# Two heads at a time: where in the gate units the second head's scores and both weightings stand, and output sums in two banks

## What is computed, cut to what matters

```python
h = rms_norm(x, norm)                         # 256 x 2048
q, k, v, g = h @ w_q, h @ w_k, h @ w_v, h @ w_g   # each 256 x 4096, 32 heads of 128
sc = q @ k.T * 128 ** -0.5 + bias_or_decay    # per head, masked
p = softmax(sc)
o = p @ v
x = x + (o * silu(g)) @ w_out
```

## Time and profile before

| what | value |
|---|---|
| device time, median of 3 runs | 2803.97 us (2802.63 to 2807.37) |
| the profiled execution, its own time | 2815.8 us |
| span of its records | 2814.1 us |
| PE busy | 2618.1 us, 93% |
| PE weight loads | 2283.6 us, 81% |
| DVE busy | 1823.2 us, 65% |
| ACT busy | 1303.0 us, 46% |
| POOL busy | 347.6 us, 12% |
| mean granted clock of PE | 0.966 |
| read from HBM | 437.35 MB |

### The profile page before, as it was taken

One profiled execution on the slowest core, in us unless ns is written; L12 is line 12 of the kernel. 1 busy time (PEld: TensorE's weight loads), 2 busy tenths in 40 slices (PEclk: granted clock), 3 DMA queues, 4 the chain that ended last, 5 costly groups with the idle time before them and its releaser, 6 DMA issues.

```text
span 2814.1 us, 43733 instructions
## 1 busy us (share of the span) xinstructions
PE 2618.1 (93%) x15162; PEld 2283.6 (81%) x15162; DVE 1823.2 (65%) x2629; ACT 1303.0 (46%) x2054; POOL 347.6 (12%) x375
## 2 busy tenths in 40 slices
PE   7999996888899999999999999999999999999997
PEld 6999993776788788888878888788888788888886
DVE  6888887347865656665565656666655666565565
ACT  5454446354444444444444445544444444444444
POOL 3111117231300000000000000110000101000012
PEclk9999998798999999999999999999999999999999
DMA  6666640007566565656656565557666666666672
GB/s 190 181 164 185 167 125 17 14 4 207 167 176 177 157 185 155 184 166 168 176 152 181 167 168 151 168 148 193 171 163 182 159 191 162 170 176 179 170 172 90
DMA packets 757372, 441.72 MB, mean 157 GB/s; under 512 B 28304, under 2 KB 720528, under 8 KB 757296
## 3 DMA queue, kind: packets, MB, share of 16 engines
q1 hardware_dynamic: 752016, 430.16, 54.7%
q0 software_dynamic: 5280, 10.56, 3.5%
HBM read 437.35 MB, written 3.31 MB: 157 GB/s over the span
## 4 chain that ended last, share of the span: by engine, by line
PE 61%; DVE 6%; ACT 6%; issue 3%; ACTq 0%; DVEq 0%; DMA 0%; POOL 0%; SPq 0%; POOLq 0%
PE bank L271 30%; PE bank L273 15%; PE bank L295 4%; PE bank L296 4%; PE bank L297 4%; ACT hib L231 4%; PE bank L1540 1%; ACT pr L1633 1%; DVE lob L238 1%; DVE gT L1783 1%; PE bank L1541 1%; DVE gT L1781 1%; DVE egT L1812 1%; DVE og L1814 0%; PE bank L1521 0%
## 5 line engine op out<-in xcount | busy, mean ns | idle before, releaser
L271 PE MATMUL bank<-xx,hib 128*128 128x512 f32 x3328 | 1221.2, 409 | 10.5 <-DVE lob L238 10.5
L238 DVE TENSOR_TENSOR lob<-rawb,hib 128x1024 fp32r<-128x1024 f32 x672 | 827.4, 1244 | 443.5 <-ACT hib L231 437.7
L273 PE MATMUL bank<-xx,lob 128*128 128x256 f32 x3328 | 941.3, 283 | 0.0
L231 ACT ACTIVATE hib<-rawb 128x1024 fp32r<-128x1024 f32 x672 | 699.1, 1054 | 516.6 <-PE bank L273 353.4
L271 PEld LDWEIGHTS bank<-xx,hib 128*128 128x128 f32 x3328 | 634.1, 191 | 159.7 <-DVE lob L238 11.2
L273 PEld LDWEIGHTS bank<-xx,lob 128*128 128x128 f32 x3328 | 637.3, 192 | 2.3
L271 PE MATMUL bank<-oo,hib 128*128 128x512 f32 x1024 | 367.9, 404 | 14.5 <-DVE gT L1783 12.8
L254 PE MATMUL bank<-xh,hia 128*128 128x258 f32 (+2 forms) x1040 | 299.5, 288 | 12.2 <-DVE xl L413 12.2
L255 PE MATMUL bank<-xl,hia 128*128 128x258 f32 (+2 forms) x1040 | 295.9, 284 | 0.0
L256 PE MATMUL bank<-xh,loa 128*128 128x258 f32 (+2 forms) x1040 | 294.9, 284 | 0.0
L273 PE MATMUL bank<-oo,lob 128*128 128x256 f32 x1024 | 289.4, 283 | 0.0
(11 more groups left out here) (303 smaller groups left out, 2648.2 us busy)
## 6 DMA issues: line engine op xcount, KB each, us to landing
rawb<-in_a_w_in_dram SPq DMA_DIRECT2D x256, 512.0 KB, 4.6
rawa<-in_w_in_dram SPq DMA_DIRECT2D x130, 512.0 KB, 5.0
rawb<-in_kv_w_dram SPq DMA_DIRECT2D x128, 512.0 KB, 4.6
rawb<-in_b_w_in_dram SPq DMA_DIRECT2D x128, 512.0 KB, 5.2
rawb<-in_a_w_out_dram SPq DMA_DIRECT2D x64, 512.0 KB, 5.1
rawb<-in_b_w_out_dram SPq DMA_DIRECT2D x64, 512.0 KB, 5.1
rawb<-in_w_out_dram SPq DMA_DIRECT2D x32, 512.0 KB, 5.4
table<-in_rel_dram POOLq DMA_DIRECT2D x32, 128.0 KB, 3.5
```

Of the source, the lines that this page charges most:

```text
L231: nc.scalar.activation(self.hi[(2 * at.u + h) % SPL][:], self.raw[at.u % RAW][:, h * HALF:(h + 1) * HALF], ACT.Copy).then_inc(hi_ready, 1)
L238: nc.vector.tensor_tensor(self.lo[b][:], self.raw[at.u % RAW][:, h * HALF:(h + 1) * HALF], self.hi[b][:].bitcast(F32), ALU.subtract).then_ ...
L271: nc.tensor.matmul(out, self.hi[b][:, w], both(k).rearrange("p a t -> p (a t)"), start=start and k == 0, stop=False)
L273: last = nc.tensor.matmul(out[:, 0:SEQ], self.lo[b][:, w], both(k)[:, 0], start=False, stop=stop and k == 7)
```

## The change

In each pair of heads, PE issues the second head's scores and then the first head's weighting together ahead of tile 6 of g_a's first half, the second head's transposes ahead of tile 6 of g_b's first half, and its weighting ahead of tile 6 of g_b's second half. The sums of even heads go to the bank OT and those of odd heads to FZ, which the norms' sums use between the layers, and the semaphore `og_ready` starts one higher, so that a weighting waits for the og of the head before the last. ACT copies the second head's turned probabilities after the first head's tanh and ahead of its copy of og, which is now a step of its own (`take_gated`); the splits of g_b follow both. DVE takes the second head's maxima between the two splits of g_a.

```diff
@@ buffers @@
     SC, PT, OT, FZ = psum[2:6]
+    OUTS = [OT, FZ]
@@ TensorE, weigh @@
-                            nc.tensor.matmul(OT[:, 0:SEQ], vtm[:, 0, w], pT[:, 0:SEQ], start=True, stop=False)
-                            nc.tensor.matmul(OT[:, P:SEQ], vtm[:, 1, w], pT[:, SEQ:W3], start=False,
+                            nc.tensor.matmul(OUTS[j % 2][:, 0:SEQ], vtm[:, 0, w], pT[:, 0:SEQ], start=True, stop=False)
+                            nc.tensor.matmul(OUTS[j % 2][:, P:SEQ], vtm[:, 1, w], pT[:, SEQ:W3], start=False,
                                              stop=True).then_inc(o_sum, 1)
+                        return emit
+                    def both(one, other):
+                        def emit():
+                            one()
+                            other()
                         return emit
@@ TensorE, the pair @@
-                        st.unit_wide(pe, g_a, xg, ({4: weigh(j_a)}, {0: scores(j_b, q_b, k_b)}))
-                        st.unit_wide(pe, g_b, xg, ({}, {0: turn_probs(j_b), 5: weigh(j_b)}))
+                        st.unit_wide(pe, g_a, xg, ({6: both(scores(j_b, q_b, k_b), weigh(j_a))}, {}))
+                        st.unit_wide(pe, g_b, xg, ({6: turn_probs(j_b)}, {6: weigh(j_b)}))
@@ ScalarE, gate @@
                         a(eg[:], gT[:], ACT.Tanh, scale=0.5).then_inc(gate_ready, 1)
-                        act.wait_ge(og_ready, head_no(layer, g, b, j) + 2)
+
+                    def take_gated(j):
+                        act.wait_ge(og_ready, head_no(layer, g, b, j) + 3)
                         dst = oo[:, bass.ds(b * VB + j, 1), 0, :].rearrange("p a t -> p (a t)")
                         a(dst, og[:], ACT.Copy).then_inc(oh_ready, 1)
...
-                    act.wait_ge(og_ready, head_no(layer, g, b, 0) + 1)
+                    act.wait_ge(og_ready, head_no(layer, g, b, 0) + 2)
@@ ScalarE, the pair @@
                         split(g_a)
                         exps(j_b)
                         gate(g_a, j_a)
+                        take_probs(j_b)
+                        take_gated(j_a)
                         split(g_b)
-                        take_probs(j_b)
                         gate(g_b, j_b)
+                        take_gated(j_b)
@@ VectorE, start @@
-            v_.memset(stat[:, 1:2], 0.0).then_inc(og_ready, 1)
+            for n in range(1, 3):
+                v_.memset(stat[:, n:n + 1], 0.0).then_inc(og_ready, 1)
@@ VectorE, gate @@
-                        stt(og[:], OT[:, 0:SEQ], 0.5, eg[:], ALU.mult, ALU.mult).then_inc(og_ready, 1)
+                        stt(og[:], OUTS[j % 2][:, 0:SEQ], 0.5, eg[:], ALU.mult, ALU.mult).then_inc(og_ready, 1)
@@ VectorE, the pair @@
                         evacuate(p, U_KB, k_b, kT)
-                        split(g_a)
+                        ahead(split_lo, g_a, 0)
                         maxima(j_b)
+                        ahead(split_lo, g_a, 1)
                         shares(j_b)
```

## The result

The changed kernel takes 2692.69 us (median of 4 runs, 2690.08 to 2697.28), the kernel before 2803.67 in the same comparison. The ratio is 0.9604, 95% interval 0.9587 to 0.9621: 111 us less. The forecast was 2707 with a range of 2692 to 2738, so the time lies 0.7 us above the range's lower end: the direction and the mechanism were right, and the gain was 14 us larger than the 97 of the sum.

A forecast was written before the change was run, and what follows sets the result against it. The prediction saw PE bound by waits for ACT's late pT copy and by clock falls beside them. Removing 71.9 us of wait and 25 us of clock, 97 us in all, took 2804 to 2707 us, range 2692 to 2738.

The forecast's parts named there:

- The wait of 71.9 us: PE's second-head weighting waits for ACT's pT copy, 2.25 us in each of 32 pairs; the change removes it.
- The schedule of the new order: Predicted start times of one pair's steps on PE, ACT and DVE, with pT 2.1 us before the second weighting.
- The thinnest margin: Second head's scores on PE need kT, forecast ready 0.6 us before them.
- A second bank worth nothing by itself: Weighting no longer waits for og of the head before; claimed worth nothing, as og came before PE was ready.
- Maxima between the splits: DVE's maxima between g_a's splits start exp 2.0 us earlier; probabilities ready 1.7 us before PE's transposes.
- The wait at the group ends: First projection matmul of each of 8 head groups waits for gT; claimed untouched at 12.8 us.
- The clock: Falls of PE's clock at the pair waits were expected to go: 33 us at most, 25 us taken.
- Two discounts: Clock gain cut from 33 to 29 us for the profiled run's 11.8 us excess, then by 4 for group-end falls.
- Rival 1: Clock falls stay, caused by the short fp32 matmuls or transposes around the wait; 2732 us, chance 0.14.
- Rival 2: New PE wait for kT at the second head's scores, 1 us late per pair; 2739 us, chance 0.09.
- Rival 3: ACT's pT copy still late behind gated copy or splits, wait returns in full; 2804 us, chance 0.04.
- Rival 4: Weight loads too slow for the shorter pair, PE waits at a unit's start; 2855 us, chance 0.03.

The follow-up runs named there:

- experiment 1: Kernel before with only ACT's order changed: pT copy after tanh, ahead of the gated copy and the splits of g_b; 2714.48 us, ratio 0.9669.
- experiment 2: Changed kernel with ACT's pT copy of the second head put back behind the splits of g_b; 2710.48 us, ratio 0.9644.
- experiment 5: Kernel of experiment 2 with the second weighting at tile 2 instead of 6 of g_b's second half; 2752.98 us, ratio 0.9816.
- experiment 6: Kernel of experiment 2 with the second weighting at tile 0 instead of 6 of g_b's second half; 2807.28 us, ratio 1.0014.
- experiment 3: Changed kernel with all heads' sums in one bank and the weighting waiting for og of the head before; 2695.23 us, ratio 0.9596.
- experiment 4: Changed kernel with DVE's second-head maxima put back behind both splits of g_a; 2730.3 us, ratio 0.9716.
- experiment 7: Changed kernel without PE's wait for gT of the last head at the start of a group's projection; 2684.38 us, ratio 0.9565.
- experiment 8: Kernel of experiment 1 without PE's wait for gT at the start of a group's projection; 2684.61 us, ratio 0.9571.

## Why the prediction was right, point by point

- **The wait of 71.9 us and its cause, ACT's queue.** Right. Experiment 1 removes it with ACT's order alone, experiments 2, 5 and 6 bring it back in three sizes.
- **The schedule of the new order.** Right to a few hundredths of a microsecond. On the clock of the prediction the rows after are: scores 1098.76 (forecast 1098.76), exp 1101.94 (1102.0), the probabilities 1103.96 (1104.0), transposes 1105.72 (1105.73), tanh 1105.13 (1105.1), og 1106.04 (1106.0), pT 1106.24 (1106.3), splits of g_b 1106.94 (1107.0), second weighting 1108.87 (1108.88). The thinnest margin, kT before the scores, is 1075.73 - 1075.10 = 0.63 us, forecast 0.6.
- **A second bank worth nothing by itself.** Right (experiment 3).
- **Maxima between the splits.** The margin of 1.7 us at the transposes was right. Moved back, the maxima cost a wait of 0.72 us per pair and, by way of the group ends, 37.6 us in all (experiment 4).
- **The wait at the group ends stays at 12.8 us.** Right, but the reason was incomplete. It stays because the splits of g_b became earlier along with g_b's end; had they not, it would have grown (experiment 1).
- **The clock.** The mechanism was right, and this is the term that was mis-sized. I took 25 us; the missing share fell by 34.1 us. Two discounts, 8 of the 9 us, were wrong. The 4 us for falls at the group ends alone: there were none in 32 such waits of four kernels. And the 4 us for the thought that the profiled execution's excess of 11.8 us was clock lost at these waits: the gain of the medians, 111 us, is as large as what the two traces explain, so that excess was not in this stage. Most of it lies ahead of it: in the trace of before the first values' matmul starts at 751.2 us, in the nine others at 739.4 to 744.9, and over the first 739 us the mean clock is 0.93 there and 0.95 or 0.96 in the others.
- **A term that was missing:** 5 us from the projections' tiles. Together with the clock, 9 + 5 = 14 us, the whole difference to 97. That the time is still in the range is luck: the wait and the whole missing share of the clock, 71.9 + 35.8 = 107.7 us, are less than was gained, and the 4 us that the lower end has on top were meant for rounding.
- **The rivals.** Rival 1 (the clock stays low for another reason) is refuted: the falls follow the wait's length with all matmuls in place (experiments 5 and 6). That the wait stands closer to the transposes in experiment 6, by 2 tiles instead of 4, doesn't explain them either: in the kernel before there were 5 tiles between them and 17 falls. The rule of the Trainium skill that spoke for it ("TensorE: Matmul & The Clock Gate", "Part 4: PE-mode transpose") gives no account of these falls: experiment 5 has the same transposes and none. Rival 2's wait did not come. Rival 3 is ruled out by the copy's place: 2.1 us before PE wants it. Rival 4 too: 179 GB/s over the stage, and no wait of PE for splits after 776 us. The one of 3.8 us ahead of it was 4.1 us in the trace of before.

## What to carry to other kernels

When a wait is found behind an in-order queue, look first at the order of that queue alone; here four lines on ACT did for the pair all that moving the matmuls did. Then ask what the late engine runs late next: a delay of 1.4 us that no pair felt came out at the end of each group, with the clock on top. And price a wait of PE by the distance between its neighbours' starts and by the clock after it, not by its idle time alone.

## What the runs showed of the hardware that I had not expected

- **Whether the clock falls depends steeply on the length of the wait.** At one place, with one set of instructions, 32 waits of 1.7 to 1.8 us had no fall and 18 of 32 waits of 2.4 us had one. A fall cost 1.94 us in the kernel before and 1.6 in experiment 6, where one block's second weightings are 41.07 us apart with a fall and another's 39.46 without. Length is not all, though. Which of 32 equal waits gets a fall stays open. And between the two layers, where waits of 0.8 to 1.4 us stand close together in all ten traces, the clock fell in four of them, the changed kernel's among them, and not in that of the kernel before.
- **A recorded wait is not its cost.** 0.31 us of idle time moved the next start by 0.48 us (experiment 2). The last matmul before the wait is recorded as busy for 0.28 us, while in a stream the next one starts 0.12 us after it (L273 at 1071.37 and L271 at 1071.49 in the changed kernel); the 0.16 us between these are about what the record of the wait leaves out.
- **PE runs the same tile at two rates at a full clock.** A projection's tile takes 0.3467 or 0.3533 us. With a wait of 1.7 us straight in front it was the faster one in all eight projections of the changed kernel, but in five of eight with one bank, in three of eight in experiment 2, and in two of eight in the kernel before. Without that wait it was the slower one in eight of eight in experiment 7. In experiment 8, which lacks the wait too, the first tiles of all eight projections took 0.353 us, and after the late 15th tile five of the eight went on at 0.347. So a stop of PE can switch the rate and doesn't always, and the rate then held to the end of the projection. What decides is open. At the faster rate the 3072 tiles of the stage's other wide units would take up to 3072 x 0.0066 = 20 us less than at the slower one, which wasn't tried.
